# First block of a two-block decoder on one core: attentions in one run, paired retention heads, gates a tile ahead

## What is computed

```python
h = rms_norm(x, norm_mix_g)
rq, rk, rv, rg, pv, nq, nk, nv, mq = jnp.split(h @ w_in, 9, axis=-1)      # 256 wide each: 4 heads of 64
ret  = merge(rms_norm(bidirectional_retention(rope(rq) / 8, rope(rk), rv, decays))) * silu(rg)
pool = multiscale_pool(pv, pool_w, pool_scale)                            # windows 2, 4, 8, 16, mixed by group
na   = neighbourhood_attention(rms_norm(nq), rms_norm(nk), nv, na_rpb)    # 8 rows x 16 columns, bias, softmax
mk, mv = jnp.split(rms_norm(mem, norm_mem_g) @ w_mem_kv, 2, axis=-1)      # 256 memory rows
mo   = memory_attention(rms_norm(mq), rms_norm(mk), mv)
up   = einsum([ret, pool, na, mo], w_branch)                              # 4 branches, 256 -> 1024 each
x    = x + (sigmoid(h @ w_gate) * up).sum(over branches) @ w_out
x    = x + swiglu(rms_norm(x, norm_ffn_g))
```

## Time and profile before

| | |
|---|---|
| median of the runs | 3418.88 us (3418.48 to 3425.0) |
| the profiled execution's own time | 3431.3 us |
| its span, first to last instruction | 3429.5 us |
| TensorE matmul busy | 3184.1 us (93%) |
| VectorE, ScalarE, GpSimd busy | 1407.7 (41%), 745.5 (22%), 1971.1 us (57%) |
| mean granted TensorE clock | 0.948 of full |
| first layer of block one, mixer | 40.02 to 546.49 us; feed-forward to 964.40 |
| second layer, mixer | 964.40 to 1469.24 us |

### The profile page before, as it was taken

The page is one execution under the profiler, slowest core; times in us unless marked ns, Lnnn a source line. Parts: engine busy times, 40 slices in busy tenths (PEclk is TensorE's granted clock), DMA queues, the critical chain, the costliest instruction groups (busy, mean ns, idle before and its releaser), DMA issues.

```text
span 3429.5 us, 44533 instructions
## 1 busy us (share of the span) xinstructions
PE 3184.1 (93%) x14188; PEld 2470.1 (72%) x14188; DVE 1407.7 (41%) x2310; ACT 745.5 (22%) x1516; POOL 1971.1 (57%) x1528
## 2 busy tenths in 40 slices
PE   5797999999978899999999778989999999999998
PEld 4554887888766458878887555878888776878886
DVE  4545334312364452254424545552114554452223
ACT  3421112100234211021002335241001333230001
POOL 4234666767662256667768231757678543747765
PEclk8897999999988889999999889999999999999999
DMA  4111223222231122222223110322223211312222
GB/s 151 38 44 56 92 92 108 94 98 98 86 111 37 43 69 93 98 89 99 98 98 107 37 65 19 102 74 98 93 98 105 74 56 51 110 65 95 98 98 86
DMA packets 78347, 284.97 MB, mean 83 GB/s; under 512 B 8688, under 2 KB 9200, under 8 KB 77424
## 3 DMA queue, kind: packets, MB, share of 16 engines
q1 hardware_dynamic: 74736, 269.41, 23.5%
q10 hardware_dynamic: 3456, 13.50, 1.1%
HBM read 280.78 MB, written 2.10 MB: 82 GB/s over the span
## 4 chain that ended last, share of the span: by engine, by line
PE 54%; DVE 6%; ACT 2%; issue 1%; DVEq 0%; ACTq 0%
PE pd L512 26%; PE pa L512 24%; PE pd L656 1%; PE po L681 1%; DVE pair L180 1%; ACT work L176 1%; PE pa L664 1%; DVE work L184 1%; DVE b_lo L180 1%; DVE work L200 1%; DVE t L188 0%; PE pd L575 0%; DVE h_lo L188 0%; PE pa L541 0%; DVE x_res L180 0%
## 5 line engine op out<-in xcount | busy, mean ns | idle before, releaser
L465 POOL TENSOR_SCALAR w_hi<-w_raw 128x1024 fp32r<-128x1024 f32 x508 | 549.2, 1081 | 1386.6 <-PE pa L512 870.5
L512 PE MATMUL pa<-h_hi,w_hi 128*128 128x512 f32 x1888 | 761.6, 403 | 25.3 <-issue 22.9
L512 PE MATMUL pa<-h_lo,w_hi 128*128 128x512 f32 x1888 | 745.7, 395 | 0.0
L512 PE MATMUL pa<-h_hi,w_lo 128*128 128x512 f32 x1888 | 744.9, 395 | 0.0
L469 POOL TENSOR_TENSOR w_lo<-w_raw,w_hi 128x512 fp32r<-128x512 f32 x508 | 742.5, 1462 | 0.0
L467 POOL TENSOR_TENSOR w_lo<-w_raw,w_hi 128x512 fp32r<-128x512 f32 x508 | 701.6, 1381 | 42.4
L512 PE MATMUL pd<-b_hi,w_hi 128*128 128x512 f32 x1152 | 457.8, 397 | 24.7 <-DVE b_lo L180 21.6
L512 PEld LDWEIGHTS pa<-h_hi,w_hi 128*128 128x128 f32 x1888 | 361.6, 192 | 129.5 <-issue 50.2
L512 PE MATMUL pd<-b_lo,w_hi 128*128 128x512 f32 x1152 | 453.0, 393 | 0.0
L512 PE MATMUL pd<-b_hi,w_lo 128*128 128x512 f32 x1152 | 452.3, 393 | 0.0
L512 PEld LDWEIGHTS pa<-h_lo,w_hi 128*128 128x128 f32 x1888 | 362.0, 192 | 77.4 <-issue 3.9
(11 more groups left out here) (154 smaller groups left out, 3309.6 us busy)
## 6 DMA issues: line engine op xcount, KB each, us to landing
w_raw<-in_w SPq DMA_DIRECT2D x508, 512.0 KB, 3.2
mrg<-in_mem ACTq DMA_DIRECT2D x4, 1024.0 KB, 4.8
mrg<-in_nabias ACTq DMA_DIRECT2D x2, 2048.0 KB, 8.7
x_res<-in_x SPq DMA_DIRECT2D x8, 256.0 KB, 5.3
out_y<-mrg ACTq DMA_DIRECT2D x8, 256.0 KB, 2.1
mrg<-in_count ACTq DMA_DIRECT2D x2, 512.0 KB, 3.8
kbuf<-in_delta ACTq DMA_DIRECT2D x2, 448.0 KB, 8.2
rope<-in_rope SPq DMA_DIRECT2D x1, 512.0 KB, 11.9
```

The lines of the kernel that those rows point to most:

```text
L465: nc.gpsimd.tensor_scalar(w_hi[:, j], raw[:, j % RR], 1.0, 1.0, ALU.mult, ALU.mult).then_inc(rounded, 1)
L512: ins = mm(out, a, b, start=(first and k == 0 and e == 0), stop=(last and k == k_n - 1 and e == 2))
```

## The change

The first block's mixer is put in another order on all engines, with the same arithmetic on nearly every operand.

- `FRONT` gives SyncE the order in which the layer's rows of the weight array are loaded; the two zero chunks of each layer aren't loaded or split (504 chunks instead of 508).
- `before_front`: three query chunks, memory keys and values with norms and one transposition. `front`: memory and neighbourhood attention are one run of 16 steps of two tiles and two trailing ones; its table `beside` gives each step at most one chunk or two (15 in all: the neighbourhood keys, values and queries, the retention's queries, keys, values and gates, the pool's two inputs `Cp`), the norms, rotations, and decay tables (`D` on VectorE, `X` the exponential on ScalarE). The distances are loaded on ScalarE's queue in the first step (`Dl`). The four decay tables get places of their own in `b_all`, the memory of `b_hi`/`b_lo`, and `mrg`.
- Queries and keys that are normed stay in `qbuf`/`kbuf` instead of passing through `qs`.
- `retention`: both heads of a pair in a step, nine steps for both pairs; `BESIDE_RET` puts the gate chunks of tile 0 (`Z`), steps of the pool's window sums on VectorE (`P`), and the head norm of the first pair (`Es`, `E`) between them. The silus of the gates come in one go before it.
- The pool's group products are scaled as they leave PSUM.
- `gates`: the gate chunks of tiles 1 to 7 come before the branch chunk of the tile ahead of theirs; VectorE multiplies a gate by the norm into `work` as soon as it is there, the sigmoid is in place; three additions; the sum is split in `m_hi`/`m_lo` tile by tile, in memory of their own, and `residual` reads them. The next layer's memory is loaded after `residual`.

The core of the diff:

```diff
+FRONT = [0, 1, 7, 4, 2, 3, 5, 8, 6, 9, 10, 12, 13, 15, 16, 17, 11, 19, 14, 18, 20, 21, 24, 25, 26, 27]
+for _m in range(1, KT):
+    FRONT += [24 + 5 * _m + b for b in range(4)] + [23 + 5 * _m]
+FRONT.append(23 + 5 * KT)
+LAYER = chunk_counts()[0]
+NLOADED = NCHUNK - 2 * (24 + 5 * KT - len(FRONT))
...
+def before_front(mem, na):
+    return [(mem, 0, "Cq"), (mem, 1, "Cq"), (na, 0, "Cq"), (mem, 0, "Nq"), (mem, 0, "Km"), (mem, 1, "Nq"),
+            (mem, 0, "Vm"), (na, 0, "Nq"), (mem, 0, "Nk"), (mem, 1, "Vm"), (mem, 0, "Tm"), (mem, 1, "Km")]
+def front(mem, na):
+    beside = [
+        [(mem, 0, "Dl"), (mem, 1, "Tm"), (mem, 1, "Nk"), (na, 0, "Ck")],
+        [(na, 0, "Nk"), (na, 0, "Cv")],
+        [(na, 0, "Tv"), (na, 1, "Cq")],
+        [(na, 1, "Nq"), (na, 1, "Ck")],
+        [(na, 1, "Nk"), (RET, 0, "Cq"), (RET, 0, "D")],
+        [(RET, 0, "Ck"), (RET, 0, "Rq"), (RET, 0, "X")],
+        [(RET, 0, "Cg"), (RET, 0, "Rk")],
+        [(RET, 1, "D")],
+        [(RET, 1, "X"), (RET, 1, "Cq")],
+        [(RET, 1, "Ck"), (RET, 1, "Rq")],
+        [(na, 1, "Cv"), (RET, 1, "Rk")],
+        [(na, 1, "Tv")],
+        [(RET, 1, "Cg")],
+        [],
+        [(RET, 0, "Cv")],
+        [(RET, 0, "Tv"), (RET, 1, "Cv")],
+        [(RET, 1, "Tv"), (RET, 0, "Cp"), (RET, 2, "D")],
+        [(RET, 1, "Cp"), (RET, 2, "X"), (RET, 3, "D")],
+    ]
+    tiles = [(ph, p, a) for ph in (mem, na) for p in range(ph.pairs) for a in range(len(ph.tiles))]
+    for s in range(0, len(tiles) + 4, 2):
+        if s < len(tiles):
+            for what in "SN":
+                for one in (s, s + 1):
+                    yield (what, *tiles[one])
...
+BESIDE_RET = ([("Z", 0), ("X", 3)], [("P", 3)], [("Z", 1), ("P", 2)], [("P", 3)], [("Z", 2), ("P", 2)],
+              [("Es", 0), ("P", 2)], [("Z", 3), ("E", 0)], [("P", 9)], [])
...
-        dtab = (qbuf[:, 2:4].rearrange("p a n -> p (a n)"), mrg[:, 4:6].rearrange("p a n -> p (a n)"))
...
+        dtab = tuple(two.rearrange("p a n -> p (a n)")
+                     for two in (b_all[:, KT + 2:KT + 4], b_all[:, 0:2], mrg[:, 6:8], b_all[:, 2:4]))
...
+                item = {}
+                for i in range(2 * ST + 1):
+                    if i < 2 * ST:
+                        p, kt = divmod(i, ST)
+                        if kt == 0:
+                            pe.wait_ge(qk_full, n.at("qk_full", n.ready.pop(("ret", p))))
+                        for j in range(2):
                             bank = bank_d()
+                            item[i, j] = n.n["pd_done"] - 1
                             n.take("pd_full")
                             r = slice(HD * j, HD * j + HD)
-                            mm(bank[:, :], kbuf[r, p % 2, P * i:P * i + P], qbuf[r, p % 2], start=True, stop=True)\
+                            mm(bank[:, :], kbuf[r, p, P * kt:P * kt + P], qbuf[r, p], start=True, stop=True)\
                                 .then_inc(pd_full, 1)
-                            n.ret_item = (n.ret_item[1], n.n["pd_done"] - 1) if a else (None, n.n["pd_done"] - 1)
-                        if nxt and a in (0, 2, 3, 4, 5, 6, 7):
-                            piece(ph, p + 1, nxt.pop(0))
-                        if a >= 1:
-                            j, i = divmod(a - 1, ST)
-                            item = n.ret_item[0] if a < 8 else n.ret_item[1]
+                    for what, k in BESIDE_RET[i]:
+                        beside_ret(what, k)
+                    if i >= 1:
+                        p, kt = divmod(i - 1, ST)
+                        if kt == 0:
+                            pe.wait_ge(*n.po_release[p])
+                        pe.wait_ge(pd_done, n.at("pd_done", item[i - 1, 1]))
+                        for j in range(2):
                             n.take("pv_done")
-                            if a == 1 and n.po_release[p % 2]:
-                                s_, v_ = n.po_release[p % 2]
-                                pe.wait_ge(s_, v_)
-                            pe.wait_ge(pd_done, n.at("pd_done", item))
-                            mm(po[p % 2][HD * j:HD * j + HD, :], vbuf[:, (p % 2) * 512 + i * P + HD * j:
-                                                                       (p % 2) * 512 + i * P + HD * j + HD],
-                               sm[:, (a - 1) % 2], start=(i == 0), stop=(i == ST - 1)).then_inc(pv_done, 1)
-                    n.po_release[p % 2] = (rt_full, n.at("rt_full", n.take("rt_full")))
+                            a = 512 * p + kt * P + HD * j
+                            mm(po[p][HD * j:HD * j + HD, :], vbuf[:, a:a + HD], sm[:, 2 * ((i - 1) % 2) + j],
...
             def gates():
+
+                for b in range(4):
+                    piece(RET, b, "Z")
+                    if b == 0:
+                        beside_ret("Es", 1)
+                        pool_products()
+                        beside_ret("E", 1)
+                wait_splits()
...
-                    if not last:
-                        four_gates()
...
+                    if m + 2 < KT:
+                        for b in range(4):
+                            piece(RET, b, "Z")
...
-                residual(B, prepare=True, each=True)
+                residual((m_hi, m_lo), prepare=True, each=True)
...
+                    for b in range(4):
+                        d = full_d(b == 3)
+                        v.tensor_tensor(gate[b], pd[d % RD][:, :], gate[b], ALU.mult).then_inc(pd_done, 1)
+                    dve.wait_ge(pd_done, n.last("pd_done"))
+                    chain(v.tensor_tensor(gate[0], gate[0], gate[1], ALU.add))
+                    chain(v.tensor_tensor(gate[2], gate[2], gate[3], ALU.add))
+                    v.tensor_tensor(mrg[:, m], gate[0], gate[2], ALU.add).then_inc(mrg_full, 1)
+                    if m + 2 < KT:
...
+                            rooted(gate[b])
+                    if m:
+                        lo(m_lo[:, m - 1], mrg[:, m - 1], m_hi[:, m - 1])
+                lo(m_lo[:, KT - 1], mrg[:, KT - 1], m_hi[:, KT - 1])
...
-                memory(Phase("mem", 2, 6, {"q": sgain[:, 1:2], "k": col(f"a{l}_mk")}), f"a{l}_mem")
-                na = Phase("na", 2, 4, {"q": sgain[:, 0:1], "k": col(f"a{l}_nak")})
-                attend(Phase("mem", 2, 6), after=na.prepare(0))
-                dve.wait_ge(aux_in[0], 16 * (l + 1))
-                dve.wait_ge(aux_in[2], 16 * (l + 1))
-                decay_table(0, 0)
-                attend(na, True, RET.prepare(0))
-                n.ret_pv = n.n["pv_done"]
+                memory_norm(f"a{l}_mem")
+                stream_norm()
+                mem = Phase("mem", 2, 6, {"q": sgain[:, 1:2], "k": col(f"a{l}_mk")})
+                na = Phase("na", 2, 4, {"q": sgain[:, 0:1], "k": col(f"a{l}_nak")}, l)
+                n.pool, n.pool_item = pool_steps(l), []
+                for one in before_front(mem, na):
+                    piece(*one)
+                run(front(mem, na))
```

## The result

The changed kernel takes 3322.47 us (median of four, 3321.36 to 3322.92) against 3419.02; the ratio is 0.9713, 95% interval 0.9696 to 0.973. That is 96.5 us less, where 131 were forecast (3288); 3322.47 lies inside the range, but 34 us from the forecast.

The account below looks back on a forecast made before the run. TensorE's idle time, low clock and serial work in the mixers were taken as the bound; 42.5 + 129.6 + 27.4 + 222.7 + 18 = 440.2 for 506.47. Two layers save 131 off the median: 3288, range 3240 to 3340.

Parts of the forecast that it names:

- 0.4% over the median of 3418.88, which I take for the comparison: Whole kernel: the 131 us saving, read from the profiled execution of 3431.3, was taken off the median, giving 3288.
- I take 2: Before the first score: the 7.52 us wait on the last memory key shrinks to 2, 5.5 less.
- The wait on the split memory (4.62) stays at 4: Before the first score: ScalarE's and VectorE's splits are the same, so this wait falls only 0.6 us.
- forecast 129.6: Run of two attentions, first layer: 121.1 us of TensorE work plus 8.5 of waits.
- forecast 27.4: Retention, first layer: 20 us with sums and pool products, waits of 2.2, and 5.2 behind the head norm.
- the pairing does nothing: Rival in the retention: two heads' 512-column products don't overlap, 15.6 us a layer return, 3319; chance 0.05.
- the last tile's own sum and split: Gates' end: this replaces the 3.96 us wait before the output projection and costs 3.3.
- VectorE binds: Rival: 28 two-input operations of seven roots at joints take 1.57 instead of 0.69 us, 24.6 a layer, 3337; chance 0.20.
- The clock neither stayed up nor down: Rival in the mixers: the clock stays up despite short waits, giving back 18 us a layer, 3252; chance 0.14.
- the four spells of 10: Mixer clock: four low-clock spells of 10 us are left, each costing about 4.5, 18 us a layer.
- Slower: Rival: clock stays at its lower level through the attentions' run and the retention, 114 us a layer more, 3516; chance 0.05.
- the signs: Profile after: no wait over 5 us, pairs 1.1, first score at 42, gate tile 27.4, mixer 440, clock 0.96, second block unchanged.

Follow-up runs that it names:

- x5: Changed kernel with the scratch of VectorE's eight head roots before and in the two attentions in PSUM instead of SBUF: 3313.42 us.
- x6: x5 with the memory norm's root in PSUM too, for the eight scalings of memory rows in each layer: 3300.98 us.
- x1: Changed kernel with the first memory key's root ahead of the first neighbourhood query's root, on VectorE alone: 3324.12 us.
- x9: Changed kernel with x2, x3 and x6 together, plus x1's order on VectorE: 3274.55 us.
- x7: Changed kernel with the memory attention's trailing transposes and outputs finished before the neighbourhood attention's first scores, two runs in place of one: 3329.45 us.
- x4: Changed kernel with the two heads' retention matmuls apart again, score then value product of one head, then the other: 3339.6 us.
- x2: Changed kernel with the first pair's head norm on VectorE after the last decay products and pool pieces instead of before: 3308.7 us.
- x3: Changed kernel with the last tile's gate chunks placed two and two behind the third last and second last branch chunks: 3309.54 us.

## Why the forecast was right in kind and 34 us too low

**The comparison, 12 us.** Two profiled executions are 108.8 us apart in span (3429.5 and 3320.7), the medians 96.5. The forecast read 131 out of the profiled execution's stages and then took it off the median. The profiled execution was 12.3 us over its median at a clock of 0.948, and the shorter ones that I could compare ran at 0.950 to 0.956: part of the half-speed spells that I counted as saved were probably in that execution and not in the median one. No trace of a median execution of the kernel before was kept, so this isn't shown. What speaks for it: outside the two mixers that execution took 2418.19 us, and the changed kernel's, which is at its median, 2419.41, so the excess hardly lies there. The step that failed is "0.4% over the median of 3418.88, which I take for the comparison"; by this reading 3300, the forecast for that execution, was the one to keep. The spread of the kernel before, 3415.7 to 3434.4, was not to be seen from three runs; the changed kernel's eight runs lie within 2.8 us.

**Before the first score, 7 and 14 us of waits.** The stage was forecast 10.5 us shorter in each layer, and is 3.0 shorter in the first and 0.5 longer in the second. This is the other step that failed. "I take 2" for the wait on the first key was wrong: 9.24 and 9.56. I priced one root, 4.2 to 5.5, and not what stands before it on VectorE, the roots of three queries, which the new order had put there; and two of them took 6.4 and 6.1 because GpSimd was splitting the memory chunks meanwhile. "The wait on the split memory (4.62) stays at 4" failed in the second layer (10.94), where the kernel before had waited 8.20; I had read that wait in the first layer only. In the first it is 3.41, and that is in part luck: in eight profiles with the same code up to there it lies between 2.14 and 6.75. x5 and x6 show the cause: shorter operations shorten both waits (9.24 and 9.56 to 5.66 and 5.23, 10.94 to 7.43). x1 and x9 show that the order of the roots doesn't shorten the total.

**The two attentions: right.** In the first layer 139.64 us at a clock of 0.94; half speed for an eighth of it costs about 8, which leaves 131 for the forecast 129.6. TensorE idles 7.7 (139.64 − 131.92), forecast 8.5. Its longest waits are 1.73 at a key's square sum and 1.48 and 1.96 in and behind a step whose tiles VectorE was late with. That the joint is cheap also holds, x7. (The 1.53 that the forecast gave for a decay table's second half is the pool's row; the table's own is 1.15.)

**The retention: right in kind, 4 us short.** From its first score to the end of the pool's products it is 61.37 us; less five chunks at 5.59 and some 2 for the half-speed spell at 276.80 to 283.60 (4.24 busy) that leaves 31.3 for the forecast 27.4. The undisturbed pairs take 1.06 and 1.01 (forecast 1.10 and 1.05), so the rival "the pairing does nothing" is out; the delays inside three pairs, 2.1 in all, weren't foreseen. The pool's pieces, priced at 1.53, took 0.68 to 1.68, 0.93 in the mean. The wait behind the head norm was seen and priced at 5.2; it is 6.80. Undoing the pairs costs less than they were priced (8.4 and 12.2 for 15.6, x4), since VectorE's pace hides a part of it. I listed that wait as a cost and did not see that it was an order of one list; x2 takes it away.

**The gates: half right.** A tile takes 27.20 to 27.45 us, as before (27.42). The 3.3 that was forecast for "the last tile's own sum and split" missed the bank: two branch chunks follow each other after the sixth tile, both `pd` banks wait for VectorE's products, and these stand behind the three additions and the split of the tile before: 4.11, and the clock behind it. x3 shows it.

**The rivals.** "VectorE binds" (0.20) was the right mechanism at the wrong places: it bound before the first score, behind the head norm and at the gates' end, and not at seven joints. The rule of the Trainium skill, "SBUF — State Buffer", "SBUF: two separate sides", that a VectorE operation with two memory inputs and a GpSimd operation reading memory shut each other out, agrees with the trace in kind: 1.31 against 0.70 us, and 0.69 with an input in PSUM. The rows that the forecast named for it, 70.38 and 71.17, are of two different operations; the same operation at both durations is `pair<-rope,pair`, 1.34 at 72.85 and 0.69 at 81.73. The clock neither stayed up nor down: 0.95 and 0.96, 45 and 36 us at half (448.88 × 0.05 / 0.5, 452.41 × 0.04 / 0.5). That is close to the four spells of 10 in sum, but not in kind: in the first mixer it is seven stretches of 3.4 to 10.2 us. "Slower" is out, transposes or not: from 96.00 to 157.00 the run of the attentions, with transposes in its steps, stood at 1.00. Of the signs, the pairs, the gate tile, the clock and the second block came as written; a wait over 5 us stood in the retention (6.80), the first score came 50 and 55 us after the first chunk, not 42, and the mixers took 448.9 and 452.4, not 440.

The sum by layer: forecast 66.3 and 64.6, measured 57.6 and 52.4, 21 short; the rest of the program took 1.2 us more. With the 12.3 of the comparison that is the 34.

## What to carry to other kernels

When a step is moved ahead of a critical result, price the whole queue that then stands before that result on the engine that makes it, in every layer, and not the last item of it. Where that queue was full, a new order of it only moved the wait here, and shorter operations shortened it: where GpSimd works beside it, one of a VectorE operation's inputs in PSUM halved its time here. And subtract a gain read from one profiled execution from that execution, and look at its clock before setting it against a median.

## What the hardware did that I had not expected

The output's place doesn't matter, the inputs' do: `po<-pair,rope`, two SBUF inputs and a PSUM output, took 1.58 us beside GpSimd, `po<-po,pair` 0.70. The same short wait was followed by the lower clock at one time and not at another: behind the wait of 1.48 the next chunk took 5.58 us in the first layer (145.28 to 150.87, clock 1.00) and 7.20 in the second (1016.32 to 1023.52, clock 0.76), with the same instructions. Removing a wait can give more than the wait: two waits of 4.11 at the gates' end gave 13.0 us, of which the windows show 11.4, by the clock behind them. And in the kernel before the clock was 0.50 through 26 us in which TensorE did single-head matmuls without a pause, 268.29 to 294.27.
